# Two-block transformer kernel in f32: the first projection's 256-column item by plain products, token half by token half

## The reference

```python
u = rmsnorm(h, norm_mix_g[l]) @ w_in[l]                  # (512, 1024) @ (1024, 3328)
o_sb = sb_group(u[..., :SB_IN], sb_out_g[l])             # attention: q, k, v, 512 columns each
o_rw = rwkv7_group(u[..., SB_IN:], shift_mu[l], ...)     # r, k, v (512 each) and xw, xa, xg (64, 64, 128)
```

## Time and profile before

| | |
|---|---|
| median of 3 runs | 1460.3 us (1455.28, 1463.12, 1460.3) |
| span of the profiled execution, first to last instruction | 1458.0 us |
| device time of the profiled execution itself | not given with the results |
| PE busy | 1346.8 us, 92% of the span |
| DVE, ACT, POOL busy | 500.6, 369.4, 313.7 us |
| first 36 us: PE busy | 21.57 us |
| mean granted TensorE clock | 0.972 of full |

### The profile page before, as it was taken

The page is one execution under the profiler, slowest core; times in us unless marked ns, Lnnn a source line. Parts: engine busy times, 40 slices in busy tenths (PEclk is TensorE's granted clock), DMA queues, the critical chain, the costliest instruction groups (busy, mean ns, idle before and its releaser), DMA issues. The chain is left out here.

```text
span 1458.0 us, 27226 instructions
## 1 busy us (share of the span) xinstructions
PE 1346.8 (92%) x11948; PEld 869.5 (60%) x11948; DVE 500.6 (34%) x906; ACT 369.4 (25%) x682; POOL 313.7 (22%) x357
## 2 busy tenths in 40 slices
PE   6999989888899999998969999998899899999995
PEld 4878764577745554454448878895545654444442
DVE  4367425442233321111283167654523201000016
ACT  2223026444133011111142241324423011111112
POOL 8436202255000200000023523440000301111100
PEclk9999999999999999999979999999999899999998
DMA  5911100300062799999941121103062589999983
GB/s 160 342 68 58 58 1 0 117 4 5 4 249 101 280 416 417 415 418 417 411 170 59 58 79 37 59 2 116 1 248 103 209 325 376 387 378 387 381 330 148
DMA packets 75596, 284.08 MB, mean 195 GB/s; under 512 B 15217, under 2 KB 16568, under 8 KB 63186
## 3 DMA queue, kind: packets, MB, share of 16 engines
q1 hardware_dynamic: 68464, 267.47, 47.4%
q0 software_dynamic: 5440, 10.58, 2.1%
q10 hardware_dynamic: 1570, 4.24, 0.7%
HBM read 259.41 MB, written 29.84 MB: 198 GB/s over the span
## 5 line engine op out<-in xcount | busy, mean ns | idle before, releaser
L2396 PE MATMUL banks<-arena_moe,mixT 128*32 128x256 f32 x1280 | 113.5, 379 | 0.0
L391 POOL TENSOR_TENSOR arena_mix<-ring 128x512 f32<-128x512 f32 (+1 forms) x56 | 72.8, 1317 | 173.4 <-PE banks L426 128.3
L436 ACT ACTIVATE arena_mix<-banks 128x256 f32<-128x256 f32 x108 | 41.1, 383 | 258.4 <-PE banks L426 258.4
L1921 POOL DMA_INDIRECT expert_rows<-arena_moe x21 | 20.5, 978 | 388.5 <-ACT arena_moe L2220 161.3
L1648 PE MATMUL banks<-ring,mixT 128*128 128x512 f32 x224 | 99.1, 595 | 3.9 <-PEq L50 3.1
L426 PE MATMUL banks<-ring 128*128 128x256 f32 x432 | 100.1, 380 | 2.7 <-DVE arena_mix L447 1.6
L426 PEld LDWEIGHTS banks<-ring 128*128 128x128 f32 x432 | 81.2, 190 | 16.5 <-issue 5.8
L1962 DVE TENSOR_TENSOR mixT<-banks,params 128x512 f32<-128x512 f32 (+1 forms) x64 | 39.9, 625 | 143.3 <-PE banks L1937 85.3
L447 DVE SCALAR_TENSOR_TENSOR arena_mix<-banks,arena_mix 128x256 f32<-128x256 f32 x81 | 33.1, 422 | 160.2 <-ACT arena_mix L436 90.0
L1937 PE MATMUL banks<-G_moe,x_hi_moe 128*128 128x256 f32 (+1 forms) x320 | 81.3, 294 | 2.9 <-issue 2.9
L426 PE MATMUL banks<-ring,arena_mix 128*128 128x256 f32 x336 | 78.7, 389 | 2.8 <-POOL arena_mix L391 1.9
(11 more groups left out here) (453 smaller groups left out, 2564.1 us busy)
## 6 DMA issues: line engine op xcount, KB each, us to landing
ring<-in_w_in SPq DMA_DIRECT2D x26, 1024.0 KB, 7.7
arena_moe<-in_exp_w_gate SPq DMA_DIRECT2D x16, 1024.0 KB, 12.4
arena_moe<-in_exp_w_up SPq DMA_DIRECT2D x16, 1024.0 KB, 16.4
arena_moe<-in_exp_w_down SPq DMA_DIRECT2D x16, 1024.0 KB, 16.0
ring<-in_exp_w_gate SPq DMA_DIRECT2D x16, 1024.0 KB, 11.7
ring<-in_exp_w_up SPq DMA_DIRECT2D x16, 1024.0 KB, 14.3
ring<-in_exp_w_down SPq DMA_DIRECT2D x16, 1024.0 KB, 17.7
arena_moe<-in_w_gate SPq DMA_DIRECT2D x8, 2048.0 KB, 11.7
```

Of the source, the lines that this page charges most:

```text
L391: pool.tensor_tensor(out[:, c], a[:, c], b[:, c], op).then_inc(ph.sem("weight_sums"), 1)
L436: act.activation(self.dest(n, i)[block], self.m.banks[a][:, 0:256], ACT.Copy, scale=self.scale(n)).then_inc(ph.sem(name), 1)
L1921: pool.indirect_dma_start(z.d.outputs, bass.IndirectOffsetOnAxis(ap=place[:, c:c + 1].bitcast(U32), axis=0), z.y[:, 2 * c:2 * c + 2, :].re ...
L2396: last = pe.matmul(hb[u][T * k:T * (k + 1), 256 * part:256 * part + 256], z.xe[:, j, at:at + T], both[:, part, j, half * 256:half * 256 + ...
```

## The change

X1 is no longer part of the seven-product scheme. It is computed by plain accumulation over the eight 128-row chunks of the input width, by a new function on PE:

```diff
+            def low_project(c, half, chunks):
+
+                if c == 0 and half == 0 and chunks[0] == 0:
+                    pe.wait_ge(ph.sem(f"ring{X1 % 2}"), 32)
+                    pe.wait_ge(ph.sem("normed"), NORMED // 2)
+                w = item_view(m, X1, ITEMS1[X1][1])
+                tokens = slice(256 * half, 256 * half + 256)
+                for k in chunks:
+                    last = pe.matmul(m.banks[6 + c][:, tokens], w[:, k, c * P:(c + 1) * P], m.mixT[:, k, tokens],
+                                     start=(k == 0), stop=(k == DC - 1), skip_group_check=True)
+                if half == 1:
+                    last.then_inc(ph.sem("low_projected"), 1)
```

There are two column groups c and two token halves; each pair is eight matmuls of 128x256, 32 in all. The order on PE becomes:

```diff
-            norm_first_pe(pe, ph, m, x.scaled)
+            for t in range(3):
+                norm_first_pe(pe, ph, m, x.scaled, t)
+            low_project(0, 0, range(DC // 2))
+            norm_first_pe(pe, ph, m, x.scaled, 3)
+            low_project(0, 0, range(DC // 2, DC))
+            low_project(1, 0, range(DC))
             pe.wait_ge(ph.sem("normed"), NORMED)
-            for p in FIRST1:
-                if p == (X1, 0, 3):
-                    pe.wait_ge(ph.sem("vectors"), 16 * len(VECTORS))
-                    pe.transpose(m.banks[7][:, 0:NVEC - GAIN_ROWS], x.raw[0:NVEC - GAIN_ROWS, :],
-                                 m.ident[0:NVEC - GAIN_ROWS, 0:NVEC - GAIN_ROWS]).then_inc(ph.sem("vectors_turned"), 1)
-                product(*p)
-            for p in PAIRS1[1:]:
-                product(V1, *p)
-            for n in range(K1, VB1 + 1):
+            for c in range(2):
+                low_project(c, 1, range(DC))
+            pe.wait_ge(ph.sem("vectors"), 16 * len(VECTORS))
+            pe.transpose(m.banks[5][:, 0:NVEC - GAIN_ROWS], x.raw[0:NVEC - GAIN_ROWS, :],
+                         m.ident[0:NVEC - GAIN_ROWS, 0:NVEC - GAIN_ROWS]).then_inc(ph.sem("vectors_turned"), 1)
+            for n in range(V1, VB1 + 1):
                 for k, p in enumerate(PAIRS1):
+                    if n == V1 and p == (1, 7):
+                        pe.wait_ge(ph.sem("vectors_taken"), 1)
                     product(n, *p)
```

ACT copies the two banks whole instead of X1's four blocks, DVE has no corners of X1, POOL has no weight sums of X1, and SP loads K1 into X1's half of the ring when X1's plain products are done:

```diff
-            kept(X1, (0, 1), (0, 6), (0, 5))
-            kept(V1, (0, 1))
-            kept(X1, (0, 3))
-            kept(V1, (1, 1), (0, 6), (1, 6), (0, 5), (1, 5), (0, 3), (1, 3))
+            for c in range(2):
+                act.wait_ge(ph.sem("low_projected"), c + 1)
+                act.activation(x.x[:, c, 1:], m.banks[6 + c][:], ACT.Copy).then_inc(ph.sem("low_taken"), 1)
+            kept(V1, (0, 1), (1, 1), (0, 6), (1, 6), (0, 5), (1, 5), (0, 3), (1, 3))
...
-            corners(X1, (0, 2), (0, 7), (0, 4))
             shift(X1)
...
             def first_sums():
-                sums(X1)
                 sums(V1)
...
             for n in range(2, len(ITEMS1)):
-                sp.wait_ge(ph.sem("product"), max(seven.done(*p) for p in ORDER1 if p[0] == n - 2))
+                if n == 2:
+                    sp.wait_ge(ph.sem("low_projected"), 2)
+                else:
+                    sp.wait_ge(ph.sem("product"), max(seven.done(*p) for p in ORDER1 if p[0] == n - 2))
```

More of the change, by code:

```diff
@@ L290, with norm_first_pe @@
 NORMED = 2 * NT
[L293 to L304, removed]
+def norm_first_pe(pe, ph, m, scaled, t):
+    pe.wait_ge(ph.sem("scaled"), t + 1)
+    for half in range(2):
+        k = 2 * t + half
+        if k >= 6:
+            pe.wait_ge(ph.sem("normed"), k - 5)
+        for j in range(4):
+            c = 4 * half + j
+            last = pe.transpose(m.banks[k % 6][:, j * P:(j + 1) * P], scaled[:, t, c * P:(c + 1) * P], m.ident[:])
+        last.then_inc(ph.sem("turned"), 1)
 def norm_first_dve(dve, ph, m, rows, scaled, gain, v):
@@ L336, with __init__ @@
 class Seven:
-    def __init__(self, m, ph, xt, ext, view, order, pair, rows_form, banks, before, dest, scale):
-        self.m, self.ph, self.view, self.order = m, ph, view, order
+    def __init__(self, m, ph, xt, ext, view, order, pair, rows_form, banks, before, dest, scale, first=0):
+        self.m, self.ph, self.view, self.order, self.first = m, ph, view, order, first
         self.rows_form, self.banks, self.before, self.dest, self.scale = rows_form, banks, before, dest, scale
@@ L385, in weight_sum @@
             if half == 0:
-                if user and n:
+                if user and n > self.first:
                     pool.wait_ge(ph.sem("product"), max(self.done(n - 1, i, user) for i in range(2) if (n - 1, i, user) in self.place))
                 if k:
-                    pool.wait_ge(ph.sem("weight_sums"), 8 * n + 2 * k)
+                    pool.wait_ge(ph.sem("weight_sums"), 8 * (n - self.first) + 2 * k)
             c = slice(2 * half, 2 * half + 2)
@@ L398, in product @@
         needs_weights = {7: 2, 5: 4, 6: 6, 3: 8}.get(j)
-        if needs_tokens and n == 0:
+        if needs_tokens and n == self.first:
             pe.wait_ge(ph.sem("token_sums"), needs_tokens)
         if needs_weights:
-            pe.wait_ge(ph.sem("weight_sums"), 8 * n + needs_weights)
+            pe.wait_ge(ph.sem("weight_sums"), 8 * (n - self.first) + needs_weights)
         old = self.before(r)
@@ L526 @@
 KEPT = (1, 6, 5, 3)
-FIRST1 = [(X1, 0, 1), (X1, 0, 2), (X1, 0, 7), (X1, 0, 6), (X1, 0, 5), (V1, 0, 1), (X1, 0, 3), (X1, 0, 4)]
-ORDER1 = FIRST1 + [(V1, i, j) for i, j in PAIRS1[1:]] + [(n, i, j) for n in range(K1, VB1 + 1) for i, j in PAIRS1]
+ORDER1 = [(n, i, j) for n in range(V1, VB1 + 1) for i, j in PAIRS1]
 def load_item1(sp, m, io, n, sem):
@@ L561, in pair @@
     def pair(n, i):
-        return max(2 * n - 1, 0) + i
+        return 2 * (n - V1) + i
     def dest(n, i):
-        buf, second = targets[n], 1 if n == X1 else 2
+        buf, second = targets[n], 2
         low, high = slice(0, 256), slice(256, 512)
@@ L572, in phase_project1 @@
                   lambda r: (3 * (r % 2), 3 * (r % 2) + 1, 3 * (r % 2) + 2), lambda r: r - 2 if r >= 2 else None, dest,
-                  lambda n: 0.125 if n == Q1 else 1.0)
+                  lambda n: 0.125 if n == Q1 else 1.0, first=V1)
     with nc.Block() as block:
@@ L661, in _ @@
             dve.wait_ge(ph.sem("vectors_turned"), 1)
-            v.mark(dve.tensor_copy(m.params[:, GAIN_ROWS:NVEC], m.banks[7][:, 0:NVEC - GAIN_ROWS]))
+            dve.tensor_copy(m.params[:, GAIN_ROWS:NVEC], m.banks[5][:, 0:NVEC - GAIN_ROWS]).then_inc(ph.sem("vectors_taken"), 1)
+            dve.wait_ge(ph.sem("vectors_taken"), 1)
             dve.wait_ge(ph.sem("small"), 2)
@@ L677, in shift @@
                 buf, first = shifted[n]
-                done = pair(n, 1 if n else 0) + 1
-                for name in ("c11", "c22", "c21", "corner"):
-                    dve.wait_ge(ph.sem(name), done)
+                if n == X1:
+                    dve.wait_ge(ph.sem("low_taken"), 2)
+                else:
+                    for name in ("c11", "c22", "c21", "corner"):
+                        dve.wait_ge(ph.sem(name), pair(n, 1) + 1)
                 for c in range(buf.shape[1]):
```

## The result

In six runs each, the changed kernel took 1447.03 us at the median (1443.78 to 1451.5), the kernel before 1458.98 us (1455.28 to 1467.35). The ratio is 0.9912, 95% interval 0.9887 to 0.9936: faster by 0.9%.

The account below looks back on a forecast made before the run. TensorE bounds the kernel, with waits in the first stage: 3.6 us earlier start, minus 1.7 added matmuls, minus 1.0 transposes, plus 6.5 of waits gives 7.4; 1460.3 - 7.4 = 1452.9 us, range 1447.5 to 1458.0.

Parts of the forecast that it names:

- Steps 1 to 5: TensorE's first stage: start 13.05, plain products 13.8 us, last transposes 1.0, vectors 0.2, V1 24.2; K1 starts at 52.3.
- Costed at nothing: First-stage work on POOL, ACT, DVE and SP said to hold up nothing; V1's sums 12 us, done at 31.
- A: Rival: a half-clock stretch moves into the plain products and costs 1.3 us; gain 6.1 us, 1454.2 us; chance 0.13.
- B: Rival: gain given back in the first block's experts, DMA engines full; gain 0 to 3.7 us, 1456.6 to 1460.3; chance 0.08.
- C: Rival: X1's weights land late, so plain products lose the early start; gain 3.8 us, 1456.5 us; chance 0.05.
- D: Rival: all plain products run at half clock, K1 at 67.1, 7.4 us later than before; 1467.7 us; chance 0.05.
- the last of the working: End of the sum: K1's 7.4 us earlier start taken off the whole run, 1460.3 - 7.4 = 1452.9 us.
- rival E: Over the run, the shifted schedule meets one or two half-clock stretches of 1.3 us fewer; 1450 to 1451.5 us; chance 0.14.

Follow-up runs that it names:

- pad_k1: The changed kernel with 17 needless 128x256 matmuls ahead of K1's first product; 1458.84 us, ratio 0.9989 to the kernel before.
- idle_k1: The changed kernel with TensorE held idle ahead of K1 until V1's mixing is done; 1460.71 us, ratio 1.0009 to the kernel before.
- kk_late: The changed kernel with R1's four small sums put two products later; 1447.15 us, ratio 0.9926 to the kernel before.
- fill: The kernel before with 2, 4 and 1 needless matmuls in the waits ahead of X1's products 7, 6 and 5; 1458.93 us, ratio 0.9991.
- reorder: The kernel before with V1's products (0,1) and (0,2) moved between X1's 2 and 7, no plain products; 1456.11 us, ratio 0.9971.
- late_plain: The changed kernel with all plain products behind the four tiles' transposes and all of normed; 1459.05 us, ratio 0.9988 to the kernel before.
- control: The kernel before, unedited, measured and profiled a second time; 1462.88 us, ratio 1.0001.

## Why the prediction was wrong

The time lies half a us below the range. The direction and the mechanism of the stage were right, and the sum for the stage came out to 0.1 us.

- *Steps 1 to 5.* Start 13.07 (13.05 forecast), last transposes 14.87 (14.8), vectors 27.93 (27.9), V1 28.14 (28.1), K1 52.41 (52.3). DVE ended the rows at 14.12 + 2.68 = 16.8 (16.6 to 16.7), covered as argued.
- *Costed at nothing.* V1's sums took 12 us as estimated. The pair beside the token sums took 3.77 us and the next, beside the end of them, 3.35, against 2.49 alone, so what the prediction cites on the shared interfaces held in kind. K1's load went out at 28.03 (27.9), R1's 2.6 us behind V1's end (2).
- *Rivals A to D.* B did not happen: the experts run with the same DMA share as before, and the changed kernel is 8.7 us ahead in them (480.03 against 488.70). C and D did not happen either. A shows in pad_k1's profile, with 0.8 us, and not in the changed kernel's.
- *The step that failed* is the last of the working: the shift of the stage was taken for the whole change of the time. In the sum the half-clock time stands at nothing, as a draw that could go either way, and rival E gave it one or two stretches, 1.3 us each, as a side case with 0.14. The six runs of the first measurement had 59 us of half-clock time at the mean, against 77 for the kernel before over the 89 runs of the later jobs: 17.5 us less, by the fit 6.1 us of time, more than twice E's upper end of 2.6. Over all 25 runs it is 9.9 us less, or 3.5 us. A further 1.3 us of the miss is the base: the forecast stands on 1460.3 us, the median of three runs, and that of six is 1458.98. With 3.5 us in the sum the forecast would have been 1460.3 - 7.4 - 3.5 = 1449.4 us, and the result well inside its range.
- *A smaller slip.* The range's upper end does not follow from its words: C with the same 2.5 us is 1459.0, not 1458.0.
- *Why it is less* is open. A wait on TensorE is followed by half clock in idle_k1 (0.50 behind 6.36 us), and by slow matmuls in six of the eleven profiles with a wait of some 3 us at one and the same place, kk_late's among them; in the other five it is not. The stretch that the old trace showed at 25 us came behind such waits, but not in the second profile of the same kernel. Whether the first stage's density also lowers the half-clock time later in the run stays open: fill, reorder and pad_k1 speak for it, late_plain against it, and the mean of 6 to 12 runs has an error of about 3 us. That the first measurement had the most of this effect is luck as far as the runs tell: the second and third, 1451.06 and 1454.64 us, lie inside the range.
- *The chances.* Faster by over 0.5% had 0.45, and it was. All three measurements lie close to or beyond that line (0.9%, 0.6%, 0.5%).

## What to carry to other kernels

A wait of the engine that bounds the kernel can cost more than its length: at one and the same wait of some 3 us the matmuls behind it ran slow in six of eleven profiles, and at full speed in the other five. Price a removed wait at its length (5.5 us expected, 5.7 found at equal half-clock time), and put the clock into the range, with the scatter that the runs of the old kernel show. Where work that needs no preparation exists (plain products, another item's first products), put it where the prepared operands are not ready yet, even if it costs 1.7 us more of matmuls; and before reformulating, try the order alone, which here gave 3.4 of the 7.3 us for two moved products. Where runs scatter with the granted clock, fit the time against it: that took the uncertainty of the change's own effect down to 0.5 us.

## What was not expected of the hardware

- The time of one and the same kernel follows its granted clock: over the 89 runs of the kernel before the correlation is -0.81, from 1472.9 us at a clock of 0.964 to 1456.6 at 0.980. The twelve runs at 0.976 still spread from 1454.3 to 1464.0 us. By the fit, a us of half-clock time costs 0.35 us of run time, less than the 0.5 us that an array busy throughout would lose.
- One and the same wait of some 3 us is followed by slow matmuls in some profiles and by matmuls at full speed in others, of the same kernel too: 2.41 us for the four records in the changed kernel's first profile, 1.99 in its second and third.
- Three of DVE's small instructions on the vectors took 0.96, 1.25 and 1.08 us in the control's profile, where the first profile of that kernel had 0.84, 0.29 and 0.17. The transpose that they need had ended 1.4 us sooner, and X1's corners behind them still came 0.6 us later, at 35.16 instead of 34.53; X1's last product waited 2.55 us instead of 0.56, and K1 stood 0.6 us later. DVE's timeline of the control:

```profile
31.76 0.96 DVE L664 TENSOR_SCALAR centre<-same 128x128 f32<-128x128 f32 x1
32.76 1.25 DVE L665 TENSOR_TENSOR centre<-centre,ident 128x128 f32<-128x128 f32 x1
34.05 1.08 DVE L666 TENSOR_SCALAR arena_mix<-params 128x4 f32<-128x4 f32 x1
```
